# Four small moves in a two-block transformer kernel: modulation tiles over more slabs, context steps that take turns with banks, low parts one step later, head sums inside a gate's product

## The chip, the cores and the metric

The kernel runs on one core of a Trainium2 chip. The metric is the device time of one execution in microseconds (us), as a median over runs.

## The reference

The reference runs two blocks one after the other, in float32, for 512 tokens of width 1024. What matters here, cut to its core:

```python
# first block, layer l of 2: 256 context tokens beside 512 latent ones
mod_lat = silu(c) @ w_ada[l] + b_ada[l]             # six shift/scale/gate vectors; the same for ctx
h = modulate(rms_norm(x, g_mix[l]), sh1, sc1)
p = softmax(qn @ kn + qr @ kr); o_a = p @ va                      # 8 heads
p = softmax(q1 @ k1) - lam * softmax(q2 @ k2); o_b = p @ vb       # 4 heads
y_b = (rms_norm(o_b, g_sub) * (1 - lam_init)) @ w_br_b
merged = sigmoid(ga) * (o_a @ w_br_a) + sigmoid(gb) * y_b         # two gates
x = x + gate * (merged @ w_out);  x = x + gate2 * conv_ffn(h2, p)
# second block, layer l of 2: projections, scores of an index, then
o_a = attention over the 256 best keys                            # 8 heads, causal
o_b = gated linear attention;  o_c = pools
x = x + concat(o_a, o_b, o_c) @ w_out;  x = x + conv_glu_ffn(...)
```

In layer 0 of the first block context queries attend to the 256 context keys, and latent queries to all 768. In layer 1 there are latent queries only.

## The kernel before

**Weights.** All weights stream from HBM as slabs of 128 x 1024, in the order of use. A slab is split into a high and a low part, and a product is three matmuls (`product`, L677 to L679). The high part is ScalarE's (`split_high`, L1461), the low part VectorE's (`split_low`, L2054). There are two places for raw slabs and two for split ones: slab n is split when slab n-2 has been used. SyncE's queue issues the loads.

**Order.** The five engines have programs written out by hand, and meet on semaphores. TensorE is in order, and so are VectorE and ScalarE: a wait holds up all that stands behind it.

**Modulation.** The vectors `mod` for later stages are sums over rows of `ada_w`, made on VectorE tile by tile (`ada_tiles`, L2240: one instruction for each tile and vector). `ADA_AFTER` says how many tiles stand behind the low split of which slab of layer 0; slabs 15 to 18 are used in the first attention, 19 to 22 in the token-major product that makes `vB` behind it. ScalarE copies `vB` out only when the whole group is done (`mod_ready`). Two more groups lie in the down products of layer 0's feed-forward, one in each half: 32 tiles of one vector, then 16 of two. There `BOTH_DOWN` = 11 slabs are used, and a group is dealt out over the closings of slabs by `len * closed // (BOTH_DOWN - 4)`.

**First block's attention** (`attend2`; `attn_a` with two maps for a step, `attn_b` with one difference). Layer 0 has 24 steps each: for each of four heads or pairs, two context steps of 256 keys, and four steps of 768. Scores lie in PSUM banks 0 and 1 for the first map, 2 and 3 for the second. A step: scores on TensorE (L1036 to L1041, L1064), minima on VectorE (L2381), exponentials on ScalarE (L1641), scaling on VectorE (L2413, L2432 to L2435), turning on TensorE (L994), values. Between them TensorE computes pieces of other products (`fills`). `next_scores` lets the next scores start only when both exponentials of this step are done.

**Head sums** (`mixed`, behind the second attention). ScalarE squares the four heads of `o_b`; TensorE sums them (`norm_sums`, L721, matmuls with one column) between the first and the second gate product; VectorE and ScalarE make the reciprocal roots while the second gate product runs; TensorE spreads them (`norm_spread`, L732), two heads at a time. ScalarE's order is gate 0, root, gate 1, high parts of two heads.

**Second block's attention** (`dsa`). 16 steps: four pairs of heads, four row tiles each with 1 to 4 key tiles. Behind each four steps the finished pair is split: ScalarE `high` (L1949), VectorE `mix_low` (L2131). Turning is L1362, values L1373, minima L2835, scaling L2842 and L2845, the copy out L2851.

Of the kernel before, what the change touches and what calls it, by code (L numbers as in the profile page):

```python
# [17 lines left out]
P = 128  # L18
# [41 lines left out]
BANK = 512  # L60
# [57 lines left out]
ADA_AFTER = {**{n: 2 for n in range(2, 8)}, 8: 1, 9: 1, **{n: 2 for n in range(10, 15)}, 21: 5, 22: 3}  # L118
# [109 lines left out]
def steps_of(l):  # L228

    ctx = [(P * t, CTX) for t in range(CTX // P)] if l == 0 else []  # L230
    return [(j, c, nk) for j in range(4) for c, nk in ctx + [(CTX + P * t, TOK) for t in range(QT)]]

# [89 lines left out]
def build(nc, wstream, ada_w, c_in, params, x_in, rope_tab, pos_in, cnt_in, ada_first, c_cols, out):  # L322
# [3 lines left out]
    with ctx:  # L326
# [255 lines left out]
        def _(sp):  # L582
# [47 lines left out]
            for group, first in ((2, DOWN_AT[0]), (3, DOWN_AT[1])):  # L630
                load_turns(end // RAW_SLOTS, first // RAW_SLOTS)
                ahead, tiles, n = first + RAW_SLOTS, len(ADA_GROUPS[group]), 0
                end = -(-(ahead + BOTH_DOWN) // RAW_SLOTS) * RAW_SLOTS
                for g in range(first // RAW_SLOTS * RAW_SLOTS, end):
                    reload(g // RAW_SLOTS, g % RAW_SLOTS)
                    if g == ahead:
                        load_c(group)
                    if g >= ahead:
                        upto = ADA_SLOTS[group] + tiles * max(g - ahead - RAW_SLOTS, 0) // (BOTH_DOWN - 4)
                        for _ in range(min(upto, tiles) - n):  # L640
                            load_tile(group, n)
                            n += 1
                assert n == tiles
# [8 lines left out]
        def _(pe):  # L652
# [290 lines left out]
            def attend2(l, two, scores, values, fills):  # L943
# [22 lines left out]
                def next_scores(i):  # L966
                    if i + 1 < n:
                        pe.wait_ge(p_ready, exped.now() + 2 * (i + 1))
                        scores(steps[i + 1])
# [58 lines left out]
            def attn_a(l):  # L1028
                wait_rot()

                def scores(step):
                    j, c, nk = step
                    c -= TOK - SEQS[l]
                    for a, k0, n in pieces(nk):
                        r = slice(NOPE * a, NOPE * a + NOPE)
                        nc.tensor.matmul(ps[:, 2 * a + k0 // BANK, 0:n], qn[l][r, j, c:c + P], kn[l][r, j, k0:k0 + n],  # L1036
                                         start=True, stop=False)
                    for a, k0, n in pieces(nk):
                        h = 2 * j + a
                        r = slice(ROPE_A * (h % 4), ROPE_A * (h % 4) + ROPE_A)  # L1040
                        mm = nc.tensor.matmul(ps[:, 2 * a + k0 // BANK, 0:n], qr[l][r, h // 4, c:c + P],  # L1041
# [58 lines left out]
            def mixed(l):  # L1100
# [19 lines left out]
                gate()  # L1120
                tiles = norm_sums([(1, own_tokens(l, G))] * H_B, sumB[l])
# [34 lines left out]
            def keep_busy(times):  # L1156

                for _ in range(times):
                    nc.tensor.matmul(ps[:, IDLE_BANK, :], col("ident", 0, P), par[:, 0:BANK], start=True, stop=True)

            def chunk_norm(groups, sums, first=0, busy=True):
                tiles = [(c0 - first) // P + t for c0, n in groups for t in range(n // P)]
                sq.add(DC * len(groups))
                keep_busy(2 if busy else 0)
                chunk_sums(sums, tiles, (DC - 1) * len(groups))
                keep_busy(1 if busy else 0)
# [262 lines left out]
        def _(act):  # L1429
# [201 lines left out]
            def attend2(l, two, fills):  # L1631
# [3 lines left out]
                def exps(i):  # L1635
# [3 lines left out]
                    for a in range(2):  # L1639
                        act.wait_ge(s_max, maxed.now() + 2 * i + a + 1)  # L1640
                        nc.scalar.activation(prob[l][i % 2][:, a, 0:nk], banks(2 * a, nk), ACT.Exp, bias=st[:, a:a + 1],  # L1641
# [391 lines left out]
        def _(dve):  # L2033
# [339 lines left out]
            def attend2(l, normalise, output, fills):  # L2373
# [230 lines left out]
            def ffn_both(l):  # L2604
# [18 lines left out]
                for half in range(2):  # L2623
# [9 lines left out]
                    for m in range(DC):  # L2633
                        for t in range(m * HALF, (m + 1) * HALF):
                            if t % SLAB_TILES == SLAB_TILES - 1 and t < DC * HALF - 1:
# [6 lines left out]
                                if closed == BOTH_DOWN - 3:  # L2642
# [183 lines left out]
            def dsa(l):  # L2826
# [32 lines left out]
                for i in range(n):  # L2859
# [3 lines left out]
                    if i:  # L2863
                        out_tile(i - 1)
                        if i % QT == 0:
# [352 lines left out]
```

## Time and profile before

| | |
|---|---|
| median of 3 runs | 3587.82 us (3587.49 to 3588.64) |
| profiled execution, its own time | 3586.76 us |
| its span | 3584.9 us |
| granted TensorE clock, mean share of full speed | 0.984 |
| TensorE busy | 3448.0 us (96%) |
| VectorE busy | 2091.4 us (58%) |
| ScalarE busy | 1317.6 us (37%) |
| bytes read from HBM | 296.16 MB, 83 GB/s |

The profile shows one execution. "Busy" counts the time in which an engine had an instruction at work; a wait is the idle time ahead of an instruction, with what ended it.

### The profile page before, as it was taken

Reading aid. Unit: us, or ns where it says so; the run is one execution under the profiler, and the core shown is the slowest. Engines: PE = TensorE matmul, PEld = TensorE weight load, DVE = VectorE, ACT = ScalarE, POOL = GpSimd, SP = SyncE. Lnnn points to the kernel's source line nnn. Section 1 sums busy time; section 2 is a strip of 40 time slices with the busy share of each in tenths; the row PEclk is TensorE's granted clock in tenths of the full one; section 3 lists DMA queues with packets and bytes.
Section 4 is the critical chain, followed back from the end, with each engine's and each line's share of the span. In section 5 each row is a group of like instructions: output and inputs, shape, how many; then the busy total and the mean of one; then the engine's idle time right before and its main releaser. Section 6 shows DMA issues by size and latency. Waiting matters only on the chain.

```text
span 3584.9 us, 46029 instructions
## 1 busy us (share of the span) xinstructions
PE 3448.0 (96%) x18212; PEld 2751.1 (77%) x18212; DVE 2091.4 (58%) x3287; ACT 1317.6 (37%) x2084; POOL 124.1 (3%) x70
## 2 busy tenths in 40 slices
PE   6999999999999989999999999998999999899998
PEld 5866778878888877667777888775888887678887
DVE  5945663455575575455546665595566549656643
ACT  3444343333213313444433333435322234532222
POOL 0000000000000000000000000150000006000000
PEclk9999999999999999999999999998999999999999
DMA  6400212111351232101132233320223332123332
GB/s 257 154 18 30 71 31 88 59 55 63 116 201 65 97 120 71 42 19 42 54 94 80 95 95 103 94 83 19 83 94 94 103 102 80 36 65 94 94 100 94
DMA packets 79221, 300.56 MB, mean 84 GB/s; under 512 B 8784, under 2 KB 8912, under 8 KB 77904
## 3 DMA queue, kind: packets, MB, share of 16 engines
q1 hardware_dynamic: 77760, 291.47, 25.1%
q10 hardware_dynamic: 1296, 6.82, 0.5%
q8 instruction: 112, 1.84, 0.2%
q14 instruction: 53, 0.43, 0.0%
HBM read 296.16 MB, written 2.10 MB: 83 GB/s over the span
## 4 chain that ended last, share of the span: by engine, by line
PE 87%; DVE 6%; ACT 3%; DMA 2%; issue 1%; SPq 0%; DVEq 0%; ACTq 0%
PE ps L677 23%; PE ps L679 23%; PE ps L678 23%; PE ps L994 2%; PE ps L1036 2%; PE ps L1041 1%; PE ps L1064 1%; PE ps L1050 1%; PE ps L1071 1%; PE ps L939 1%; DVE ps L2240 1%; PE ps L940 1%; PE ps L941 1%; DVE ada_o L2240 1%; PE ps L695 1%
## 5 line engine op out<-in xcount | busy, mean ns | idle before, releaser
L2054 DVE TENSOR_TENSOR split<-raw,split 128x1024 fp32r<-128x1024 f32 x412 | 504.3, 1224 | 817.4 <-ACT split L1461 816.5
L1461 ACT ACTIVATE split<-raw 128x1024 fp32r<-128x1024 f32 x442 | 466.2, 1055 | 759.8 <-PE ps L679 672.0
L677 PE MATMUL ps<-h,split 128*128 128x512 f32 x1328 | 532.6, 401 | 3.5 <-DVE split L2054 2.3
L679 PE MATMUL ps<-h,split 128*128 128x512 f32 x1328 | 524.7, 395 | 0.0
L678 PE MATMUL ps<-h,split 128*128 128x512 f32 x1328 | 524.5, 395 | 0.0
L677 PE MATMUL ps<-h_hl,split 128*128 128x512 f32 (+1 forms) x776 | 295.2, 380 | 14.2 <-DVE h_hl L2134 8.7
L677 PEld LDWEIGHTS ps<-h,split 128*128 128x128 f32 x1328 | 250.6, 189 | 69.8 <-issue 7.4
L678 PEld LDWEIGHTS ps<-h,split 128*128 128x128 f32 x1328 | 250.7, 189 | 60.1 <-issue 3.4
L679 PEld LDWEIGHTS ps<-h,split 128*128 128x128 f32 x1328 | 250.6, 189 | 58.4
L679 PE MATMUL ps<-h_hl,split 128*128 128x512 f32 (+1 forms) x776 | 277.5, 358 | 0.0
L678 PE MATMUL ps<-h_hl,split 128*128 128x512 f32 (+1 forms) x776 | 277.0, 357 | 0.0
L677 PE MATMUL ps<-h2w,split 128*128 128x256 f32 (+1 forms) x704 | 239.0, 339 | 3.1 <-DVE split L2054 2.0
L678 PE MATMUL ps<-h2w,split 128*128 128x256 f32 (+1 forms) x704 | 238.3, 339 | 0.0
L679 PE MATMUL ps<-h2w,split 128*128 128x256 f32 (+1 forms) x704 | 238.0, 338 | 0.0
L677 PE MATMUL ps<-g_hl,split 128*128 128x512 f32 x528 | 208.4, 395 | 0.0
L679 PE MATMUL ps<-g_hl,split 128*128 128x512 f32 x528 | 208.4, 395 | 0.0
L678 PE MATMUL ps<-g_hl,split 128*128 128x512 f32 x528 | 208.4, 395 | 0.0
L677 PEld LDWEIGHTS ps<-h_hl,split 128*128 128x128 f32 x776 | 150.5, 194 | 53.8 <-issue 20.9
L2381 DVE TENSOR_REDUCE stat<-ps 128x1 f32<-128x768 f32 (+1 forms) x160 | 128.5, 844 | 86.2 <-PE ps L1041 81.0
L2920 POOL TENSOR_TENSOR split<-raw,split 128x1024 fp32r<-128x1024 f32 x30 | 75.0, 2499 | 2911.0 <-ACT split L1461 2910.3
L679 PEld LDWEIGHTS ps<-h_hl,split 128*128 128x128 f32 x776 | 150.1, 193 | 21.8
L1641 ACT ACTIVATE prob<-ps,stat 128x768 f32<-128x768 f32 (+1 forms) x160 | 128.7, 812 | 102.9 <-DVE stat L2381 102.9
(412 smaller groups left out, 6294.3 us busy)
## 6 DMA issues: line engine op xcount, KB each, us to landing
raw<-wstream SPq DMA_DIRECT2D x442, 512.0 KB, 3.5
ada_t<-ada_w SPq DMA_DIRECT2D x80, 512.0 KB, 4.9
first_w<-ada_first SPq DMA_DIRECT2D x4, 2048.0 KB, 24.7
x<-x_in SPq DMA_DIRECT2D x1, 3072.0 KB, 12.4
x<-x_in ACTq DMA_DIRECT2D x1, 3072.0 KB, 10.9
ada_c<-c_in SPq DMA_DIRECT2D x2, 1024.0 KB, 4.8
out<-x SPq DMA_DIRECT2D x8, 256.0 KB, 2.2
par<-params SPq DMA_DIRECT2D x1, 1345.0 KB, 5.6
```

Of the source, the lines that this page charges most:

```text
L677: nc.tensor.matmul(o, wh, a[0], start=first, stop=False)
L678: nc.tensor.matmul(o, wh, a[1], start=False, stop=False)
L679: return nc.tensor.matmul(o, wl, a[0], start=False, stop=last)
L695: nc.tensor.matmul(o, col(perm, 0, P), src, start=True, stop=True).then_inc(acc_ready, 1)
L994: mm = nc.tensor.transpose(ps[:, 4 + t // 4, (t % 4) * P:(t % 4 + 1) * P], p[:, t * P:(t + 1) * P], col("ident", 0, P))
L1036: nc.tensor.matmul(ps[:, 2 * a + k0 // BANK, 0:n], qn[l][r, j, c:c + P], kn[l][r, j, k0:k0 + n], start=True, stop=False)
L1461: nc.scalar.activation(split[:, n % SPLIT_SLOTS, 0, :], raw[:, n % RAW_SLOTS, :], copy).then_inc(hi_split, 1)
L1641: nc.scalar.activation(prob[l][i % 2][:, a, 0:nk], banks(2 * a, nk), ACT.Exp, bias=st[:, a:a + 1], scale=-1.0, accum_out=st[:, 2 + a:3 + a ...
L2054: nc.vector.tensor_tensor(split[:, n % SPLIT_SLOTS, 1, :], raw[:, n % RAW_SLOTS, :], split[:, n % SPLIT_SLOTS, 0, :].bitcast(F32), ALU.sub ...
L2240: ins = nc.vector.tensor_tensor_reduce(out=ada_out if group == 1 else banks(6, D), in0=w, in1=ada_c[group][:, j, :], scale=1.0, scalar=0.0 ...
L2381: nc.vector.tensor_reduce(st[:, a:a + 1], banks(2 * a, steps[i][2]), AX.X, ALU.min).then_inc(s_max, 1)
L2920: nc.gpsimd.tensor_tensor(split[:, n % SPLIT_SLOTS, 1, :], raw[:, n % RAW_SLOTS, :], split[:, n % SPLIT_SLOTS, 0, :].bitcast(F32), ALU.sub ...
```

## The change

Five edits, none of which adds or takes away an instruction:

- `ADA_AFTER`: slabs 17 to 20 get one tile each, slab 21 goes from 5 tiles to 2, slab 22 from 3 to 2. In the down products the divisor goes from 7 to 8, so that each group is dealt out over one more slab. The first three `keep_busy` matmuls of `chunk_norm` write bank 4 (`ACC_BANKS`) in place of bank 6.
- `odd(step)`: the second context step of each pair writes its scores one bank higher, and its scores wait for one step's exponentials fewer.
- `dsa`: `mix_low` for a finished pair stands one step later in VectorE's program.
- `mixed`: the head sums are no longer ahead of the second gate product but inside it.

```diff
-ADA_AFTER = {**{n: 2 for n in range(2, 8)}, 8: 1, 9: 1, **{n: 2 for n in range(10, 15)}, 21: 5, 22: 3}
+ADA_AFTER = {**{n: 2 for n in range(2, 8)}, 8: 1, 9: 1, **{n: 2 for n in range(10, 15)},
+             **{n: 1 for n in range(17, 21)}, 21: 2, 22: 2}
...
+def odd(step):
+
+    _, c, nk = step
+    return nk == CTX and c == P
...
-                        upto = ADA_SLOTS[group] + tiles * max(g - ahead - RAW_SLOTS, 0) // (BOTH_DOWN - 4)
+                        upto = ADA_SLOTS[group] + tiles * max(g - ahead - RAW_SLOTS, 0) // (BOTH_DOWN - 3)
...
                 def next_scores(i):
                     if i + 1 < n:
-                        pe.wait_ge(p_ready, exped.now() + 2 * (i + 1))
+                        ended = i if odd(steps[i + 1]) else i + 1
+                        if exped.n + ended:
+                            pe.wait_ge(p_ready, exped.now() + 2 * ended)
                         scores(steps[i + 1])
...
-                        mm = nc.tensor.matmul(ps[:, 2 * a + k0 // BANK, 0:n], dq[l][r, h, c:c + P], dk[l][r, h, k0:k0 + n],
+                        mm = nc.tensor.matmul(ps[:, 2 * a + k0 // BANK + odd(step), 0:n], dq[l][r, h, c:c + P], dk[l][r, h, k0:k0 + n],
...
-                gate()
-                tiles = norm_sums([(1, own_tokens(l, G))] * H_B, sumB[l])
+                def sums_of(head, first, end):
+
+                    for t in range(first, end):
+                        at = head * per + t
+                        mm = nc.tensor.matmul(ps[:, NORM_BANK, at:at + 1], sumB[l][head][:, t * P:(t + 1) * P], col("ones"),
+                                              start=at == 0, stop=at == tiles - 1)
+                    return mm
...
+                for g in G:
+                    o = open_acc(g[1])
+                    for k in range(DC):
+                        mm = product(o, w, k, cols(h_hl)(k, g), k == 0, k == DC - 1)
+                        if k == DC - 1:
+                            mm.then_inc(slab_used if g == G[-1] else acc_ready, 1)
+                        elif g == G[-1] and k >= DC - H_B:
+                            head = k - (DC - H_B)
+                            if head == 0:
+                                pe.wait_ge(var_ready, norms.now(back=1))
+                            pe.wait_ge(sq_ready, sq.now(back=H_B - 1 - head))
+                            sums_of(head, 0, per)
+                pe.wait_ge(sq_ready, sq.now())
+                sums_of(H_B - 1, 0, per).then_inc(sums_ready, 1)
                 gate()
...
-                        nc.vector.tensor_reduce(st[:, a:a + 1], banks(2 * a, steps[i][2]), AX.X, ALU.min).then_inc(s_max, 1)
+                        nc.vector.tensor_reduce(st[:, a:a + 1], banks(2 * a + odd(steps[i]), steps[i][2]), AX.X, ALU.min)\
+                            .then_inc(s_max, 1)
...
-                                end = min(len(ADA_GROUPS[group]) * closed // (BOTH_DOWN - 4), len(ADA_GROUPS[group]))
+                                end = min(len(ADA_GROUPS[group]) * closed // (BOTH_DOWN - 3), len(ADA_GROUPS[group]))
...
-                        if i % QT == 0:
+                        if i % QT == 1 and i > 1:
                             mix_low(i // QT - 1)
```

Where it moves instructions, before and after, by the order of each engine's program. Three places; line numbers after the change are higher by up to 35.

VectorE in `dsa` of layer 0, behind the first four steps, before: `p` are the maps, `mix` the heads' outputs, `mix_hl_303` the split first pair.

```order
L2851 COPY mix<-ps 128x128
L2131 TENSOR_TENSOR mix_hl_303<-mix,mix_hl_303 128x512
L2842 RECIPROCAL stat<-stat 128x2
L2845 TENSOR_SCALAR p_299<-p_299,stat 128x256 x2
L2835 ISA p_298,stat<-ps,far 128x512
```

The same place after:

```order
L2886 COPY mix<-ps 128x128
L2877 RECIPROCAL stat<-stat 128x2
L2880 TENSOR_SCALAR p_299<-p_299,stat 128x256 x2
L2870 ISA p_298,stat<-ps,far 128x512
L2870 ISA stat 128x1
L2870 ISA p_298,stat<-ps,far 128x512
L2870 ISA stat 128x1
L2886 COPY mix<-ps 128x128
L2165 TENSOR_TENSOR mix_hl_303<-mix,mix_hl_303 128x512
L2877 RECIPROCAL stat<-stat 128x2
L2880 TENSOR_SCALAR p_297<-p_297,stat 128x384 x2
```

The low part of a pair (third line from the end) now stands behind the scaling of the next step, the minima two steps on and one more copy.

TensorE in `mixed` of layer 0, between the two gate products, before: `sumB_182` to `sumB_185` are the squares of the four heads.

```order
L679 MATMUL ps<-h_hl,split 128x512
L721 MATMUL ps<-par,sumB_182 128x1 x6
L721 MATMUL ps<-par,sumB_183 128x1 x6
L721 MATMUL ps<-par,sumB_184 128x1 x6
L721 MATMUL ps<-par,sumB_185 128x1 x6
L677 MATMUL ps<-h_hl,split 128x256
```

After, at the end of the second gate product and the start of the next:

```order
L1133 MATMUL ps<-par,sumB_183 128x1 x6
L684 MATMUL ps<-h_hl,split 128x512
L685 MATMUL ps<-h_hl,split 128x512
L686 MATMUL ps<-h_hl,split 128x512
L1133 MATMUL ps<-par,sumB_184 128x1 x6
L684 MATMUL ps<-h_hl,split 128x512
L685 MATMUL ps<-h_hl,split 128x512
L686 MATMUL ps<-h_hl,split 128x512
L1133 MATMUL ps<-par,sumB_185 128x1 x6
```

The last head's sums, which release the root, now stand behind the whole second gate product in place of ahead of it.

VectorE in the first attention of layer 0, in a context step: `prob` are the maps, `ada_t` a tile of modulation weights; `ISA` with `ada_o` is L2240. Before:

```order
L2413 TENSOR_SCALAR prob_109<-prob_109,stat 128x256 x2
L2381 TENSOR_REDUCE stat<-ps 128x1 x2
L2054 TENSOR_TENSOR split<-raw,split 128x1024
L2419 COPY qn_95<-ps 128x128
L2411 RECIPROCAL stat<-stat 128x2
L2413 TENSOR_SCALAR prob_110<-prob_110,stat 128x256 x2
```

After:

```order
L2448 TENSOR_SCALAR prob_109<-prob_109,stat 128x256 x2
L2415 TENSOR_REDUCE stat<-ps 128x1 x2
L2088 TENSOR_TENSOR split<-raw,split 128x1024
L2274 ISA ada_o,mod<-ada_t_67,ada_c_64 128x1024
L2274 ISA mod 128x1
L2274 ISA ada_o,mod<-ada_t_67,ada_c_64 128x1024
L2274 ISA mod 128x1
L2454 COPY qn_95<-ps 128x128
L2446 RECIPROCAL stat<-stat 128x2
L2448 TENSOR_SCALAR prob_110<-prob_110,stat 128x256 x2
```

One tile, two vectors, now stands between a slab's low split and the copy out and scaling of the second context step, at three of the four heads, and once behind the last step.

## Rows read from the trace of the kernel before

**Rows 1.** The page's first part: busy time, share, instructions.

```profile
PE 3448.0 (96%) x18212; PEld 2751.1 (77%) x18212; DVE 2091.4 (58%) x3287; ACT 1317.6 (37%) x2084; POOL 124.1 (3%) x70
```

**Rows 2.** TensorE's waits: us in total, times, longest us.

```profile
PE ps L1362 <- DVE p L2845: 11.2, 11, 2.2
```

**Rows 3.** Stretches: length, busy of the engines, granted clock, DMA share, GB/s.

```profile
186.90:193.60 6.70, 5.96 (x26) 4.44 (x26) 2.32 (x8) 2.36 (x10) 0.00 (x0) 0.50 0.27 78
548.70:555.40 6.70, 6.70 (x32) 6.70 (x32) 1.69 (x9) 2.35 (x3) 0.00 (x0) 0.50 0.27 78
553.17:563.62 10.45, 10.45 (x59) 9.36 (x59) 0.73 (x4) 4.05 (x5) 0.00 (x0) 0.89 0.01 2
563.62:568.60 4.98, 4.98 (x34) 4.42 (x32) 4.95 (x5) 1.97 (x3) 0.00 (x0) 1.00 0.31 105
```

**Rows 4.** Timeline of `dsa`, both layers: start, us, engine, line [idle before].

```profile
2454.95 0.44 PE L1362 MATMUL ps<-par,p 128*128 128x128 f32 x2 [0.53 <-DVE p L2845]
...
2464.74 0.44 PE L1362 MATMUL ps<-par,p 128*128 128x128 f32 x2
...
2467.33 0.69 DVE L2131 TENSOR_TENSOR mix_hl<-mix,mix_hl 128x512 fp32r<-128x512 f32 x1 [2.19 <-ACT mix_hl L1949]
...
2468.81 0.66 PE L1362 MATMUL ps<-par,p 128*128 128x128 f32 x4 [2.20 <-DVE p L2845]
...
2491.08 0.44 PE L1362 MATMUL ps<-par,p 128*128 128x128 f32 x2
...
3106.91 0.44 PE L1362 MATMUL ps<-par,p 128*128 128x128 f32 x2
...
3134.39 0.44 PE L1362 MATMUL ps<-par,p 128*128 128x128 f32 x2
```

**Rows 5.** Timeline, start of layer 0's first attention.

```profile
187.64 1.22 PE L1036 MATMUL ps<-kn,qn 64*128 64x256 f32 x4 [1.62 <-ACT prob L1641]
187.82 0.62 DVE L2413 TENSOR_SCALAR prob<-prob,stat 128x256 f32<-128x256 f32 x2
...
193.55 1.59 PE L1036 MATMUL ps<-kn,qn 64*128 64x512 f32 x8
```

**Rows 6.** Timeline, the product for `vB` and the start of the second attention.

```profile
381.49 0.50 PE L939 MATMUL ps<-split,h_hl 128*128 128x512 f32 x1 [1.37 <-DVE split L2054]
...
392.39 0.70 PE L1064 MATMUL ps<-dk,dq 64*128 64x256 f32 x4 [2.24 <-ACT vB L1448]
...
396.86 1.22 PE L1064 MATMUL ps<-dk,dq 64*128 64x256 f32 x4 [2.86 <-ACT prob L1641]
...
402.28 1.56 PE L1064 MATMUL ps<-dk,dq 64*128 64x512 f32 x8
```

**Rows 7.** Modulation tiles by line: count, busy us, mean ns, idle before.

```profile
L2240 DVE CUSTOM_DVE_ANT_0 ada_o<-ada_t,ada_c 128x1024 f32<-128x1024 f32 x64 | 78.3, 1224 | 11.2 <-DMA ada_t<-ada_w 4.9 <-ACT ada_c L1552 3.6
```

**Rows 8.** Timeline, head sums and their spreads, layers 0 and 1.

```profile
544.92 6.84 PE L721 MATMUL ps<-par,sumB 128*128 128x1 f32 x48
...
553.18 1.28 ACT L1718 ACT_TABLE_LOAD   x1
...
561.86 2.84 PE L732 MATMUL ps<-par,rstd 128*128 128x128 f32 x24
...
568.77 2.84 PE L732 MATMUL ps<-par,rstd 128*128 128x128 f32 x24
...
1756.37 3.63 PE L721 MATMUL ps<-par,sumB 128*128 128x1 f32 x32
...
1772.83 1.38 PE L732 MATMUL ps<-par,rstd 128*128 128x128 f32 x10 [1.03 <-DVE oB_hl L2131]
```

**Rows 9.** Timeline, the down products of layer 0, both halves.

```profile
1001.22 0.36 PE L677 MATMUL ps<-gw_hl,split 128*128 128x256 f32 x1 [1.34 <-DVE x L2569]
...
1328.69 0.36 PE L677 MATMUL ps<-gw_hl,split 128*128 128x256 f32 x1 [3.30 <-DVE x L2569]
...
1343.68 1.47 PE L1152 MATMUL ps<-par,sumD 128*128 128x1 f32 x12 [1.47 <-DVE sumD L2173]
```

More of the change, by code:

```diff
@@ L1035, in scores @@
                         r = slice(NOPE * a, NOPE * a + NOPE)
-                        nc.tensor.matmul(ps[:, 2 * a + k0 // BANK, 0:n], qn[l][r, j, c:c + P], kn[l][r, j, k0:k0 + n],
+                        nc.tensor.matmul(ps[:, 2 * a + k0 // BANK + odd(step), 0:n], qn[l][r, j, c:c + P], kn[l][r, j, k0:k0 + n],
                                          start=True, stop=False)
@@ L1040, in scores @@
                         r = slice(ROPE_A * (h % 4), ROPE_A * (h % 4) + ROPE_A)
-                        mm = nc.tensor.matmul(ps[:, 2 * a + k0 // BANK, 0:n], qr[l][r, h // 4, c:c + P],
+                        mm = nc.tensor.matmul(ps[:, 2 * a + k0 // BANK + odd(step), 0:n], qr[l][r, h // 4, c:c + P],
                                               kr[l][r, k0:k0 + n], start=False, stop=True, tile_position=(r.start, 0))
@@ L1118, in branch_b @@
                         gemm(w, 4, 4, kept(oB_hl[l]), g, g == G[-1])
-                gate()
-                tiles = norm_sums([(1, own_tokens(l, G))] * H_B, sumB[l])
+                def sums_of(head, first, end):
[4 more added lines that the diff above has]
+                    return mm
+                per = SEQS[l] // P
+                tiles = H_B * per
+                norms.add()
+                sq.add(H_B)
+                w = open_slab()
+                for g in G:
[12 more added lines that the diff above has]
+                sums_of(H_B - 1, 0, per).then_inc(sums_ready, 1)
                 gate()
@@ L1154, in chunk_sums, with keep_busy @@
                 mm.then_inc(sums_ready, 1)
-            def keep_busy(times):
+            def keep_busy(times, bank=IDLE_BANK):
                 for _ in range(times):
-                    nc.tensor.matmul(ps[:, IDLE_BANK, :], col("ident", 0, P), par[:, 0:BANK], start=True, stop=True)
+                    nc.tensor.matmul(ps[:, bank, :], col("ident", 0, P), par[:, 0:BANK], start=True, stop=True)
             def chunk_norm(groups, sums, first=0, busy=True):
@@ L1163, in chunk_norm @@
                 sq.add(DC * len(groups))
-                keep_busy(2 if busy else 0)
+                keep_busy(2 if busy else 0, ACC_BANKS)
                 chunk_sums(sums, tiles, (DC - 1) * len(groups))
-                keep_busy(1 if busy else 0)
+                keep_busy(1 if busy else 0, ACC_BANKS)
                 norm_spread(0, len(tiles))
@@ L1640, in exps @@
                         act.wait_ge(s_max, maxed.now() + 2 * i + a + 1)
-                        nc.scalar.activation(prob[l][i % 2][:, a, 0:nk], banks(2 * a, nk), ACT.Exp, bias=st[:, a:a + 1],
+                        nc.scalar.activation(prob[l][i % 2][:, a, 0:nk], banks(2 * a + odd(steps[i]), nk), ACT.Exp, bias=st[:, a:a + 1],
                                              scale=-1.0, accum_out=st[:, 2 + a:3 + a]).then_inc(p_ready, 1)
@@ L2638, in ffn_both @@
                                     dve.wait_ge(c_ready, group + 1)
-                                end = min(len(ADA_GROUPS[group]) * closed // (BOTH_DOWN - 4), len(ADA_GROUPS[group]))
+                                end = min(len(ADA_GROUPS[group]) * closed // (BOTH_DOWN - 3), len(ADA_GROUPS[group]))
                                 ada_tiles(group, done, end - done)
                                 closed, done = closed + 1, end
-                                if closed == BOTH_DOWN - 3:
+                                if closed == BOTH_DOWN - 2:
                                     add_bias(group)
```

## The prediction

> **What bounds the kernel now.** I read the page's busy times first: TensorE is busy for 3448.0 of 3584.9 us [rows 1], so a gain can come only from its 137 us of idle time and from stretches in which it runs at half speed. Then the waits: the largest that the change touches is the turning of maps in `dsa`, which waits 11.2 us for VectorE's scaling [rows 2]. Then the granted clock of stretches: 6.7 us at 0.50 (1.2 in place of 2.4 GHz) at the start of the first attention, where TensorE was busy for 5.96 of them, and again 6.7 us behind the head sums [rows 3]. A wait that goes can thus be worth more than itself. Last the timelines around each edit [rows 4 to 9], which the sum is made from. It is made against the profiled execution (3586.76 us); the median of the runs is 1.1 us above that.
>
> **Low parts a step later: 11.5 + 1.0 us gained.** Behind four steps of `dsa` VectorE waits 2.19 us for ScalarE's high part before it makes the low one, and the next scaling is queued behind; the turning on TensorE waits 2.20 us for that [rows 4]. ScalarE makes the high part only behind its exponentials. One step later it is there. What VectorE then does in the place of the wait, scaling of step 5, needs exponentials that were done long before. The low part (0.69) stays on VectorE's path in the next step, which had 0.2 us of slack, so about 0.65 us of new delay. The first four steps, which hold no low part, give the pace: from 2454.95 to 2464.74, 9.8 us. The eight steps behind them take 26.3 us in layer 0 (2464.74 to 2491.08) and 27.5 in layer 1 (3106.91 to 3134.39) [rows 4]. Four groups at 9.8 + 0.65 are 41.8 in place of 53.8: 12.0 us, of which 6 are waits (4 x (2.2 - 0.65)) and the rest half clock behind them. If the clock falls all the same, only the 6 are left. I take 11.5, near the upper end, since the first group runs with short waits of its own at full clock. The third low part of each layer lies beside the sums of the other heads, which fill TensorE's wait already: 0.5 us each, between nothing and 2.2.
>
> **Banks in turn: 2.5 us gained in the first attention.** Only second context steps change, eight in layer 0. I went through TensorE's row in front of each: it waits only in the first pair of each attention, 1.62 us and 2.86 us [rows 5, 6]; at the other six it comes to the scores after the exponentials. So six of eight are worth nothing. In the first attention the scores then run beside the exponentials, and turning waits for the scaling that starts at 187.82 [rows 5]: it can start at about 188.2. From there the remaining pieces (12 matmuls of 256 columns, 1.4 us at full clock, and two turnings) lead to the next scores at about 190.4, where they now start at 193.55: 3.1 us. If the clock stays at half, as it does now from 186.9 [rows 3], 1.3. I take 2.5.
>
> **Modulation tiles: 5.6 us gained at the second attention, with the banks.** A tile of two vectors is 2 x 1.22 us and their steps, some 2.6 us [rows 7]. Behind slab 21's split VectorE now has five, so slab 22's low split is late and TensorE waits 1.37 us; the last tile ends late too, ScalarE copies `vB` only then, and scores wait 2.24 us; then come the 2.86 us above, partly because the low split of a slab is queued ahead of the minima [rows 6]. With two tiles each, slab 22's split ends before TensorE needs it and the group is done about 10 us (four tiles) earlier. The first scores move from 392.4 to 388.6; VectorE's queue (a copy, a high and a low split: 0.6 + 1.05 + 1.2) lets minima start at about 391.5 in place of 395.3, and the scores of the third step can start at 396.0 in place of 402.28: 6.3 us, or 4.6 if the clock falls there again. I take 5.6.
>
> **What the tiles cost where they go.** In a context step VectorE waits 1.0 us for values and has 2.7 us before its next minima; a tile of 2.6 us moves the scaling of the second context step by 1.5 us, and its turning stands behind 3 us of scores. Nothing. Queued behind the tile are the copy out and that scaling; TensorE's next value product waits for the copy 4 us later. SyncE's queue gets a tile's load between slab loads; a tile waits for the tile two before, which is used by then, and the raw slab behind it is needed 40 us later. Without that cover it would be up to 1.5 us at each of three places.
>
> **Down products: 1.3 + 2.6 us gained.** In the first half one wait of 1.34 us goes, as a slab now has 4 tiles and never 5 [rows 9]. In the second half VectorE is the pace: two or three tiles of two vectors, the split, and the residual with its sums of squares. Its work is the same, but two tiles (5.2 us) go behind the last slab that TensorE had to wait for, to where VectorE now idles 3.2 us. TensorE's wait of 3.30 goes, and the sums of squares come at 1340.1 in place of 1343.68 [rows 9]: 3.6 us. But TensorE then ends its products about 5 us ahead of those sums in place of 3, which can take the clock down for the norm behind: I take 2.6, between 0.5 and 3.6. The bank of `keep_busy` costs nothing: no one else uses bank 4 there.
>
> **Head sums: 2.2 us lost.** Now the sums end at 551.6, the table load for the next function starts at 553.18, the rest of the root is 0.7 us of VectorE, all beside the second gate product; the spread at 561.86 waits for nothing [rows 8]. In the middle lies 6.7 us at half clock [rows 3]. The sums at full clock are 0.109 us a matmul (32 in 3.49 us), so 5.2 us for layer 0. Woven in, the product (8.5 us, twice the 4.3 between the first spread's end and the second spread) and the sums end at 544.9 + 8.5 + 5.2 = 558.6. The root takes 2.4 us more: spread at 561.0, 0.8 us earlier than now. But ScalarE has gate 1 behind the root: a table load, a sigmoid, two copies and a split, 4.05 us of work [rows 3], to 564.2; then VectorE's split, scaling and low parts, 4.95 us, to 569.2, where the second spread now starts at 568.77 [rows 3, 8]. So +0.5 us; in layer 1, with a shorter product (5.6 us) and the low parts already 1.03 us late [rows 8], the same sum gives +1.6. I take 2.2, between a gain of 1 (if only the spread counted) and a loss of 4 (if the clock falls in the new gap).
> On the clock, the stretch at 0.50 behind the head sums shows TensorE busy for all of its 6.70 us, with matmuls of one column ahead of it [rows 3, 8]; so it was not idleness that took it down. The Trainium skill, "TensorE: Matmul & The Clock Gate", section "Why this matters for your kernels", names idle gaps as what to avoid. By that alone the weaving would return none of the 3.3 us that the half clock costs layer 0 now, and the loss would be 5.5 in place of 2.2; the trace speaks against it.
> On the table load, the row shows 1.28 us and the sigmoid right behind [rows 8]. The Trainium skill, "ScalarE: Activation LUTs", section "What ACT_TABLE_LOAD costs", gives about 2.66 us for a switch, with a drain. By that the loss would be 2.8 us larger over both layers; no such drain stands in this trace.
>
> **The sum.** 11.5 + 1.0 + 2.5 + 5.6 + 1.3 + 2.6 - 2.2 = 22.3 us. 3586.8 - 22.3 = 3564.5, and with the 1.1 us of the median 3565.5 us.
>
> **The rivals.** *The clock falls anyway* (0.14): `dsa` gives 6, the attentions 1.3 and 4.6, the down products 1.8, the head sums lose 4: 10 us, 3578. For it: `dsa` runs close to where the clock falls. Against: it holds through the first four steps of both layers.
> *The moves bring nothing* (0.04): the waits only move on, since `dsa`'s VectorE is the bound once the low part is on its path, and the tiles hold up attention; 3588. Against: VectorE waits several times in each group of four steps now.
> *Slower* (0.02): SyncE's queue is blocked by a tile's load in front of a slab's load in the first attention, so that TensorE runs out of slabs. It decides once it costs more than 7.4 us at each of the slabs 17 to 20 (29.5 us over four, against a gain of 22.3 and 7.2 us of margin); say 10 us each gives 3606. Against: a slab is used for some 40 us there and a load takes 3.5 to 5.
>
> **The numbers.** The forecast with its own bounds gets 0.80, 3557 to 3574. With the first rival's near side the range is 3556 to 3576 us. A measurement of this kernel can tell 0.2%, 7.2 us, from no change. Faster by more than that: 0.80 + 0.14 = 0.94; within: 0.04; slower: 0.02.
>
> **What the profile after would show.** `dsa`: no wait of 2.2 us for scaling, four steps in some 10.4 us, no half clock inside. First attention: second scores without a wait, third step's scores 3 us earlier; at the other context steps no difference. `vB`: no wait for slab 22's split, none for `vB`. Down: the last long wait for `x` gone, sums of squares 3.6 us earlier with a longer wait before them. Head sums: TensorE waits some 2.4 us for the root and 1 to 2 us for low parts. Wrong would be: half clock behind the woven sums that costs over 4 us, or VectorE late at the turnings of second context steps.

## The result and the profile after

The changed kernel takes 3553.22 us (3552.59 to 3557.43, 4 runs) against 3588.23 us (3587.49 to 3593.46) before: ratio 0.9902, 95% interval 0.9885 to 0.9919, so 29 to 41 us faster. The forecast was 3565.5 us with 3556 to 3576: the direction was right, the gain too small by 12 us, and the time lies 2.8 us below the range. The profiled executions are 33.4 us apart (3586.76 and 3553.33). Two executions on record, one of the kernel before (9248.31 us) and one of an experiment (13619.91 us), were far slower than all others and stay out of every ratio here.

The page's first part, after, answers to [rows 1]:

```profile
PE 3430.9 (97%) x18212; PEld 2738.6 (77%) x18212; DVE 2089.4 (59%) x3287; ACT 1316.8 (37%) x2084; POOL 122.6 (3%) x70
```

TensorE is busy for 17.1 us less, though its instructions are the same. It was busy for 96.2 us at half clock before and is for 58.6 after; work at half clock takes twice as long (12 matmuls of the head sums 2.55 us in place of 1.39, below), so half of the difference, 18.8 us, is what the half clock no longer takes, about the 17.1 us. The other 16 us are waits.

Timeline of TensorE after, at the starts of the two attentions, against [rows 5, 6]:

```profile
188.19 0.44 PE L1003 MATMUL ps<-par,prob 128*128 128x128 f32 x2 [0.94 <-DVE prob L2448]
...
190.22 1.56 PE L1045 MATMUL ps<-kn,qn 64*128 64x512 f32 x8
...
385.07 0.70 PE L1073 MATMUL ps<-dk,dq 64*128 64x256 f32 x4
386.61 0.70 PE L1073 MATMUL ps<-dk,dq 64*128 64x256 f32 x4
390.77 0.44 PE L1003 MATMUL ps<-par,prob 128*128 128x128 f32 x2 [1.48 <-DVE prob L2470]
392.16 1.56 PE L1073 MATMUL ps<-dk,dq 64*128 64x512 f32 x8 [0.59 <-ACT prob L1675]
```

The third step's scores stand at 190.22 in place of 193.55 (forecast: 190.4) and at 392.16 in place of 402.28. No score waits for `vB` now.

Head sums after, layer 0 and layer 1, against [rows 8]:

```profile
532.65 1.39 PE L1133 MATMUL ps<-par,sumB 128*128 128x1 f32 x12
...
539.08 2.55 PE L1133 MATMUL ps<-par,sumB 128*128 128x1 f32 x12
...
551.65 2.84 PE L739 MATMUL ps<-par,rstd 128*128 128x128 f32 x24
...
1745.36 0.95 PE L1133 MATMUL ps<-par,sumB 128*128 128x1 f32 x8
...
1751.83 1.95 PE L739 MATMUL ps<-par,rstd 128*128 128x128 f32 x16
...
1757.59 2.05 PE L739 MATMUL ps<-par,rstd 128*128 128x128 f32 x16 [1.03 <-DVE oB_hl L2165]
```

The first spread still follows a whole product behind the last sums (12.6 us after their start in layer 0, 6.5 in layer 1, with no wait). The sums are woven into the gate product that stood *ahead* of them. The text ahead of this one calls it the second gate product; that is a misreading of the diff, and the forecast rests on it.

Down products after, the waits of the second half and the norm, against [rows 9]:

```profile
1273.22 0.36 PE L684 MATMUL ps<-gw_hl,split 128*128 128x256 f32 x1 [0.97 <-DVE x L2604]
...
1296.74 0.39 PE L684 MATMUL ps<-gw_hl,split 128*128 128x256 f32 x1 [1.65 <-DVE split L2088]
...
1322.30 1.88 PE L1193 MATMUL ps<-par 128*128 128x512 f32 x4
1328.11 2.69 PE L1186 MATMUL ps<-par,sumD 128*128 128x1 f32 x12 [3.93 <-DVE sumD L2207]
1330.66 2.06 PE L1193 MATMUL ps<-par 128*128 128x512 f32 x2
```

The wait of 3.30 us for `x` is gone. Of the smaller ones, 1.57 us for a split and 0.64 for the root are gone, and one of 1.28 is down to 0.33. Behind them the wait for the sums of squares has grown from 1.47 to 3.93 us, and the sums behind it take 2.69 us in place of 1.47.

`dsa` after, layer 0, against [rows 4]:

```profile
2438.08 0.44 PE L1396 MATMUL ps<-par,p 128*128 128x128 f32 x2 [0.53 <-DVE p L2880]
...
2447.87 0.44 PE L1396 MATMUL ps<-par,p 128*128 128x128 f32 x2
...
2452.44 0.88 PE L1396 MATMUL ps<-par,p 128*128 128x128 f32 x6 [0.77 <-DVE p L2880]
...
2458.26 0.44 PE L1396 MATMUL ps<-par,p 128*128 128x128 f32 x2
...
2468.64 0.44 PE L1396 MATMUL ps<-par,p 128*128 128x128 f32 x2
```

Four steps take 10.39 us; 0.6 us late at the third step (0.77 of wait in place of 0.17) is what the low part still costs.

Stretches after (length, busy of PE, PEld, DVE, ACT, POOL, granted clock, DMA share, GB/s), against [rows 3]:

```profile
187.00:193.60 6.60, 5.66 (x39) 3.66 (x36) 2.50 (x9) 2.23 (x10) 0.00 (x0) 1.00 0.46 159
388.60:402.00 13.40, 11.32 (x64) 8.00 (x64) 8.90 (x20) 6.50 (x20) 0.00 (x0) 1.00 0.12 39
538.29:545.10 6.81, 6.81 (x32) 6.61 (x31) 2.82 (x10) 4.67 (x6) 0.00 (x0) 0.51 0.22 70
1741.40:1751.83 10.43, 10.43 (x60) 8.98 (x60) 2.73 (x10) 5.32 (x7) 0.00 (x0) 1.00 0.16 52
...
1322.30:1338.26 15.96, 10.95 (x38) 6.65 (x36) 9.76 (x20) 6.37 (x10) 0.00 (x0) 0.79 0.37 131
2438.08:2468.64 30.56, 26.43 (x228) 16.28 (x228) 24.40 (x101) 22.37 (x63) 0.00 (x0) 1.00 0.00 1
2468.64:2487.41 18.77, 15.88 (x126) 12.43 (x125) 10.28 (x31) 8.58 (x17) 0.00 (x0) 0.82 0.01 2
3101.50:3124.40 22.90, 20.07 (x134) 16.05 (x133) 11.75 (x33) 9.21 (x18) 0.00 (x0) 0.70 0.00 1
```

The clock is now full at both attentions, behind layer 1's head sums and in the first twelve steps of both `dsa` stages. In the last group of each `dsa` stage and the rows behind it, it is not (the last two rows), as before the change (0.76 and 0.71 there). It is still half behind layer 0's head sums, and newly so at the norm.

### The profile page after: what moved, and what is told of

The parts are those of the page before. It is cut to its first block, busy times and chain, and to the rows that moved or that the text cites. A ratio compares the mean times of both kernels' runs of the same rounds, so it can differ in the third digit from the quotient of the medians.

```text
span 3551.5 us, 46029 instructions
## 1 busy us (share of the span) xinstructions
PE 3430.9 (97%) x18212; PEld 2738.6 (77%) x18212; DVE 2089.4 (59%) x3287; ACT 1316.8 (37%) x2084; POOL 122.6 (3%) x70
## 4 chain that ended last, share of the span: by engine, by line
PE 89%; DVE 6%; ACT 3%; issue 1%; DMA 1%; SPq 0%; DVEq 0%; ACTq 0%
PE ps L684 24%; PE ps L686 23%; PE ps L685 23%; PE ps L1003 2%; PE ps L1045 2%; PE ps L946 1%; PE ps L1050 1%; PE ps L1073 1%; PE ps L948 1%; PE ps L947 1%; PE ps L1059 1%; PE ps L1080 1%; DVE ps L2274 1%; PE ps L702 1%; ACT split L1495 1%
## 6 DMA issues: line engine op xcount, KB each, us to landing
x<-x_in SPq DMA_DIRECT2D x1, 3072.0 KB, 12.5
```

## Experiments

Each kernel was timed beside the kernel before, and a ratio compares these two; the kernel before had medians of 3592.80 us beside the first four experiments (low parts, head sums, banks and tiles alone), 3592.64 beside the next (down products alone, the second product, nine dummies) and 3588.12 beside the last two. So the medians below are not to be held against 3588.23.

How they are read: the kernels differ by less than one timing can tell, so each trace is cut at the starts of the same TensorE instructions (before: 184.14, 205.48; 375.07, 408.40; 540.02, 575.21; 988.18, 1040.09; 1247.04, 1364.14; 1750.01, 1778.11; 2425.56, 2454.95, 2512.02; 3097.13, 3158.20), and the pieces are compared. Each piece, in us, over the profiled executions of all kernels with and without the edit in question:

```
stretch                        without the edit       with it                  forecast gain
start of the first attention   20.20-21.35 (7)        18.00-18.04 (6)          2.5
vB and second attention        33.27-33.48 (6)        banks alone 30.88; tiles
                                                      alone 26.97; both
                                                      26.53-26.60 (5)          5.6
layer 0's head sums            35.10-36.72 (6)        33.53-36.69 (6)          \ -2.2
layer 1's head sums            28.10-28.13 (6)        26.55-26.57 (6)          /
down, first half               51.89-51.92 (7)        50.09-50.17 (6)          1.3
down, second half, and norm    117.05-120.72 (7)      115.20-116.12 (3)        2.6
dsa, a group with a low part   12.17-14.57 (7 x 4)    10.38-10.39 (5 x 4)      11.5 over four
dsa, layer 0, last group       16.47-16.73 (7)        14.48 (4), 15.73         \ 1.0
dsa, layer 1, last group       17.63-18.64 (7)        17.70-17.71 (5)          /
no edit: ahead of first dsa    26.99 or 29.39-29.42 (13)
no edit: start of the program  176.78-179.88 (13)
```

The whole profiled times are no measure of one edit: 3573.89 us for low parts alone (expected 3571.5 or 3574.3), 3585.30 for head sums alone (3585.1), but 3588.49 for banks alone (3580.9) and 3585.17 for tiles alone (3577.9 to 3583.2). With banks alone the two edited stretches gave 5.8 us, as expected, while the start of the program was 2.4 us longer than in the first trace, the second half of down 3.6 and the rows from 575 to 988 us 2.6, none of them touched by that edit. The gains by single timings (18.3, 5.0, 6.5, 6.1 and 6.1 us by the ratios) add up to 42, each with an interval of 3 to 6 us to either side, too wide to tell that from the 35 of the whole change.

**Low parts alone.**

```diff
-                        if i % QT == 0:
+                        if i % QT == 1 and i > 1:
                             mix_low(i // QT - 1)
```

> Kernel before with the low parts one step later alone. If the gain seen in both dsa stages is this edit's own (in the traces of before and after the distance to the kernel before grows from 16.9 to 24.6 us in layer 0's dsa and from 26.2 to 33.8 in layer 1's): 15.3 us, 3571.5 profiled. Rival, the forecast's term: 12.5 us, 3574.3. Position theory: the first stretch at half clock (2443.0 of the kernel before) stays, since nothing ahead of it moves, and the one at 2989 goes or stays by where the stage then falls: 1.6 us more or not.

3574.52 us, ratio 0.9949 (0.9933 to 0.9966); `dsa` takes 51.56 and 53.45 us. Against the kernel before's first trace (57.07, 61.07) that is 5.5 + 7.6 = 13.1, against the mean of the seven traces without the edit (58.43, 60.19) 6.9 + 6.7 = 13.6 us: between the two numbers expected. Groups are 10.38 us each, exactly as in the changed kernel. That layer 0's stage takes 2.2 us more here than there (49.33) lies in its last group (15.73 for 14.48) and the rows behind it, at half clock for longer. From the start of the last group to the end of the stage it is 21.00 us here, 20.94 to 21.98 in the seven traces without the edit, and 18.77 to 18.78 in the two traces of the changed kernel and the two with dummies alone. So the edit alone does not show the gain that the changed kernel has there; where it comes from no run isolates.

**Head sums alone.**

```diff
-                gate()
-                tiles = norm_sums([(1, own_tokens(l, G))] * H_B, sumB[l])
+                w = open_slab()
+                for g in G:
+                    o = open_acc(g[1])
+                    for k in range(DC):
+                        mm = product(o, w, k, cols(h_hl)(k, g), k == 0, k == DC - 1)
...
+                            sums_of(head, 0, per)
...
+                sums_of(H_B - 1, 0, per).then_inc(sums_ready, 1)
                 gate()
                 norm_spread(0, tiles // 2)
```

> Kernel before with the head sums woven into the first gate product alone. If the gain belongs to this edit: 0.15 us in layer 0 and 1.55 us in layer 1 (no half clock behind the sums), 3585.1 profiled. Rival, the forecast's term: 2.2 us slower, 3589.0. Position theory: layer 1's gain depends on where the stage falls and can be 0; then 3586.6.

3587.86 us, ratio 0.9986 (0.9976 to 0.9996). Layer 0: 35.14, no gain; layer 1: 26.56, 1.55 us gained, as in all six traces with the edit. That is neither the forecast's loss nor chance: 28.10 to 28.13 without, 26.55 to 26.57 with. In the kernel before, the stretch behind those sums ran at 0.76:

```profile
1759.86:1767.07 7.21, 7.21 (x26) 5.75 (x26) 1.60 (x9) 2.13 (x3) 0.00 (x0) 0.76 0.19 73
```

The matmuls of one column stood in a row of 32 for 3.63 us [rows 8]; in pieces of 8 with products between, the clock holds (1.00 above). In layer 0, with pieces of 12, it falls as before. Why it holds in the one and falls in the other no run isolates.

**Head sums in the second gate product**, which is what the forecast had costed:

```diff
                 gate()
-                tiles = norm_sums([(1, own_tokens(l, G))] * H_B, sumB[l])
-                gate()
+                w = open_slab()
+                for g in G:
...
+                sums_of(H_B - 1, 0, per).then_inc(sums_ready, 1)
                 norm_spread(0, tiles // 2)
```

> Kernel before with the head sums woven into the second gate product, which is what the forecast had costed. By its working: 0.5 us lost in layer 0 (stretch of 35.2 us to 35.7), 1.7 lost in layer 1 (28.1 to 29.8), between a gain of 1 and a loss of 4. Rival: the root then stands in front of the spread with no cover, and the clock falls in the wait: 4 us or more lost.

3596.84 us, ratio 1.001 (1.000 to 1.002). Layer 0 39.79 us, 4.6 lost; layer 1 29.56, 1.45 lost: 6.1 us in both, against 2.2 forecast and 4 as its worst. TensorE's timeline, both layers, ScalarE's in layer 1, and a stretch of layer 0:

```profile
553.20 1.39 PE L1124 MATMUL ps<-par,sumB 128*128 128x1 f32 x12
555.25 2.55 PE L1124 MATMUL ps<-par,sumB 128*128 128x1 f32 x12
559.09 2.55 PE L1124 MATMUL ps<-par,sumB 128*128 128x1 f32 x12
563.96 5.26 PE L732 MATMUL ps<-par,rstd 128*128 128x128 f32 x24 [2.31 <-DVE rstd L2141]
...
1774.54 0.95 PE L1124 MATMUL ps<-par,sumB 128*128 128x1 f32 x8
1777.70 3.41 PE L732 MATMUL ps<-par,rstd 128*128 128x128 f32 x16 [2.21 <-DVE rstd L2141]
```
```profile
1776.83 1.28 ACT L1743 ACT_TABLE_LOAD   x1
1778.12 0.63 ACT L1743 ACTIVATE ga<-ga 128x512 f32<-128x512 f32 x1
```
```profile
555.20:568.90 13.70, 11.39 (x51) 10.96 (x50) 2.92 (x10) 4.05 (x6) 0.00 (x0) 0.50 0.01 2
```

The wait for the root is 2.31 and 2.21 us (forecast: 2.4), and layer 1's loss is the forecast's within 0.2 us. In layer 0 the costing fell short by 4.1. The clock did not fall in the new gap, as the forecast had feared, but 6.4 us ahead of it: at 555.2 us, with TensorE busy for all of 555.2 to 561.6 us, and it stayed at half for 13.7 us in place of 6.8 [rows 3]. The third and the fourth head's sums took 2.55 us each in place of 1.39, the product between them was slow too, and they ended at 561.6 and not at 558.6, and the spread behind the gap took 5.26 us in place of 2.84. In layer 1 the clock did fall in the gap (at 1777.2 us, for 3.4 us), but the fall that the kernel before has ahead of it did not come, so that the number agrees there partly by luck. The costing of the wait was sound, then, and that of the clock was not, on the place that it was meant for too.

**Banks alone** (`odd` and all its uses):

```diff
-                        pe.wait_ge(p_ready, exped.now() + 2 * (i + 1))
+                        ended = i if odd(steps[i + 1]) else i + 1
+                        if exped.n + ended:
+                            pe.wait_ge(p_ready, exped.now() + 2 * ended)
```

> Kernel before with banks in turn alone. First attention: 3.4 us earlier, as in the trace of the changed kernel. Second attention: the wait of 2.86 us goes, but minima still stand behind the copy of vB, so 2.5 us: together 5.9, 3580.9. Rival: without the tiles moved the banks bring nothing at the second attention, since minima are late: 3.4, 3583.4.

3585.93 us, ratio 0.9982 (0.9972 to 0.9992). First attention 18.02, second 30.88 (2.45 gained, as expected). The first attention without banks has two lengths, 21.35 and 20.20, by how long the clock stays at half; with them it has one. The edit is worth 2.2 to 3.3 us there.

**Tiles alone** (`ADA_AFTER`):

```diff
-ADA_AFTER = {**{n: 2 for n in range(2, 8)}, 8: 1, 9: 1, **{n: 2 for n in range(10, 15)}, 21: 5, 22: 3}
+ADA_AFTER = {**{n: 2 for n in range(2, 8)}, 8: 1, 9: 1, **{n: 2 for n in range(10, 15)},
+             **{n: 1 for n in range(17, 21)}, 21: 2, 22: 2}
```

> Kernel before with the modulation tiles over slabs 17 to 22 alone. The waits of 1.37 and 2.24 us at the vB product go; the wait of 2.86 and the half clock behind it stay: 3.6 us, 3583.2. If the clock does not fall there: 5.3 us more at most, 3577.9. Rival: tiles in attention cost something at the second context steps, up to 1.5 us at each of three: 3586 to 3588.

3586.56 us, ratio 0.9983 (0.9973 to 0.9992). The stretch takes 26.97 us: 6.4 us gained without banks. The wait for the exponentials stays, but the half clock behind it does not come:

```profile
393.31 0.70 PE L1065 MATMUL ps<-dk,dq 64*128 64x256 f32 x4 [2.74 <-ACT prob L1642]
```
```profile
385.00:400.00 15.00, 12.26 (x69) 9.07 (x68) 6.81 (x15) 6.92 (x18) 0.00 (x0) 1.00 0.18 63
```

The kernel with banks alone has it the other way round: its first two waits stay (1.53 and 2.34 us), the last is 0.59, and the clock over 385 to 400 us is 0.89. So here it fell behind the first waits, not behind the last. That rests on one trace of each kernel; that both edits together keep the clock full, on five. Banks add 0.4 us to the tiles. The rest of the first attention, in which tiles now stand, takes 169.6 to 169.8 us in all thirteen traces, with and without them: the zero that was forecast for them holds.

**Down products alone** (divisor 8, and bank 4 for the dummies):

```diff
-                                end = min(len(ADA_GROUPS[group]) * closed // (BOTH_DOWN - 4), len(ADA_GROUPS[group]))
+                                end = min(len(ADA_GROUPS[group]) * closed // (BOTH_DOWN - 3), len(ADA_GROUPS[group]))
```

> Kernel before with the divisor 8 in the down products and bank 4 for the first dummy matmuls alone. By the trace of the changed kernel: first half 1.8 us shorter (stretch of 51.9 us to 50.1), second half with its norm 1.8 shorter (117.1 to 115.3), as the 6.1 us gained ahead of the norm are partly given back at half clock behind a wait of 3.9 us. Rival: the giving back is chance of position, and here the whole second half comes out 3 us or more shorter. Time ratio 0.999 against the kernel before.

3585.82 us, ratio 0.9983 (0.9974 to 0.9993). First half 50.17, second 116.12. The wait of 4.01 us and the slow sums behind it are there too:

```profile
1339.63 2.69 PE L1152 MATMUL ps<-par,sumD 128*128 128x1 f32 x12 [4.01 <-DVE sumD L2173]
```

How much the norm gives back depends on what it is held against. From the start of these sums to the end of the stretch it is 20.46 us in the first trace of the kernel before, where the clock fell nowhere in the stretch, but 20.44 to 22.43 (mean 21.28) in the seven traces without the edit, five of which have a fall of their own; with the edit it is 22.22 to 23.01 (mean 22.50, three traces). On the means the norm gives back 1.2 us of the 4.5 gained ahead of it. The bank of the dummies stands in the same kernel and was not tried by itself.

**The same programs again.** The kernel before and the changed kernel, each unchanged:

> The kernel before, unchanged, once more with a profile. Position theory: stretches that no edit touches differ between executions of one program by 1 to 3 us each where the clock falls or not (the stretch ahead of the first dsa stage 27.0 or 29.4; dsa of layer 0 57 to 60; dsa of layer 1 59 to 61). Rival: each program has its own fixed lengths; then every stretch comes within 0.3 us of the first profile.

> The changed kernel, unchanged, once more with a profile. If its 33 us hold two or three us of chance: stretches without an edit move by 1 to 3 us (start of the program 176.9 to 179.9; ahead of the first dsa stage 27.0 or 29.4), while the edited ones stay: first attention 18.0, product for vB and second attention 26.5, layer 1's head sums 26.6, groups of four steps in dsa 10.4. Rival: everything within 0.3 us of the first profile.

3589.24 and 3553.53 us. The kernel before, again: start of the program 179.88 (176.95 at first), first attention 20.21 (21.34), second half of down 119.82 (117.10), ahead of `dsa` 26.99 (29.39), `dsa` 59.25 and 59.99 (57.07 and 61.07). So identical instructions differ by 1 to 3 us where the clock falls or not. The runs were made on several chips, but that does not explain it: on one of them the start of the program, the same in all kernels, took 176.83 us with low parts alone and 179.53 with head sums alone. The stretch ahead of `dsa`, first and second trace of the kernel before:

```profile
2435.37:2454.95 19.58, 18.39 (x233) 12.71 (x233) 9.54 (x24) 10.88 (x19) 0.00 (x0) 0.83 0.07 27
```
```profile
2438.00:2457.76 19.76, 17.15 (x237) 11.70 (x236) 11.98 (x27) 13.00 (x23) 0.00 (x0) 1.00 0.10 29
```

The changed kernel's second trace is much like its first: all edited stretches within 0.1 us, an unedited one (behind the head sums) by 1.0, another by 1.4.

**Dummies in the new wait.** Nine and, in a second kernel, four, on top of the changed kernel:

```diff
+                    keep_busy(9, ACC_BANKS)
                     chunk_norm(BOTH, sumD)
```

> Changed kernel with nine more dummy matmuls in the wait of 3.93 us for the sums of squares behind the second down half. If the half clock behind that wait comes from the idle time: the clock stays at 1.00 and the norm is 1.8 us shorter (stretch of 33.3 us to 31.5 or less), as long as the dummies (9 x 0.43 = 3.8 us) end before the sums are there. Rival: the dummies run past the sums or the clock falls anyway: 0 to 1 us longer.

> Changed kernel with four more dummy matmuls (0.86 us each, as the run with nine showed, 3.4 us in all) in the wait of 3.93 us. If idle time takes the clock down there: stretch of the second down half with its norm 115.3 us to 113.4. Rival: the dummies load the clock too little, or the clock falls all the same: 115.3, no change. Over the whole kernel 1.9 us at most, at the edge of what the timing can tell.

Nine: the second half with its norm 117.14 us (115.27 without), since a dummy takes 0.86 us and not 0.43, and they ran 3.7 us past the sums; even so only 1.9 were lost, as the clock stayed full. Four: 113.40 us, 1.9 gained, to the number expected:

```profile
1326.17 5.31 PE L1194 MATMUL ps<-par 128*128 128x512 f32 x12
1332.04 1.47 PE L1187 MATMUL ps<-par,sumD 128*128 128x1 f32 x12 [0.56 <-DVE sumD L2208]
```
```profile
1326.17:1341.00 14.83, 12.56 (x48) 6.69 (x47) 10.44 (x21) 6.44 (x10) 0.00 (x0) 1.00 0.41 141
```

The run below has the same four dummies and was traced too, and there the gain is mostly gone: 114.75 us, 0.5 less than without. The clock fell all the same, at 1335.7 us, 2.4 us after the start of the sums and with no wait over 0.63 us since the last product:

```profile
1336.40 2.93 PE L739 MATMUL ps<-par,rstd 128*128 128x128 f32 x12 [0.63 <-DVE rstd L2151]
1339.12 4.42 PE L1194 MATMUL ps<-par 128*128 128x512 f32 x6
```

So with the wait unfilled the clock fell in three traces of three, with it filled in one of three. That speaks for the idle time as a cause, which agrees with what the Trainium skill, "TensorE: Matmul & The Clock Gate", section "Why this matters for your kernels", says of gaps; it does not show it, and filling the wait is no sure cure. The whole kernels take 3556.82 and 3555.51 us, no difference that the timing can tell.

**Low parts in the long step**, with the four dummies:

```diff
-                        if i % QT == 1 and i > 1:
+                        if i in (7, 11, 13):
```

> Changed kernel with the four dummies and with the low parts of dsa behind steps 7, 11 and 13 in place of 5, 9 and 13. If the low part finds slack in the long fourth step of a group: the wait of 0.77 us behind the third step goes and the four groups take 9.8 us in place of 10.4, 2.4 us in all. Rival: the low part is in VectorE's way in any step: 10.4 again.

All four groups take 9.79 us (the third low part of a layer stays behind step 13); the third step waits 0.17 again:

```profile
2453.85 0.88 PE L1397 MATMUL ps<-par,p 128*128 128x128 f32 x6 [0.17 <-DVE p L2881]
```

The last group of layer 0 took 15.38 in place of 14.48, so 1.7 us show in the two stages (49.60 and 51.48 for 49.33 and 53.45). 3552.70 us, ratio 0.9894 (0.9877 to 0.9910): the lowest median here, and against the changed kernel's own ratio not to be told from it.

## Why the prediction missed

The profiled gain of 33.4 us by stretch, and what was forecast:

- **Head sums, +1.6 for -2.2.** The step that failed: "Woven in, the product ... and the sums end at 544.9 + 8.5 + 5.2 = 558.6". The product that now holds the sums is the one that ended at 544.9 already. The root keeps its cover and nothing is lost: that is 2.2 us of the miss. The other 1.6 are layer 1's half clock, which the forecast had not looked at. A second premise failed with it: the weaving was to give back the half clock of layer 0 (sums at 5.2 us, "3.3 us that the half clock costs layer 0 now"). It gave back nothing there (35.13 us for 35.18, the clock at 0.51 over 6.81 us); it did in layer 1. So the reading that the prediction set against its own, that weaving returns nothing, came true in layer 0 and failed in layer 1. Read rightly, with no loss, the same range would have begun at 3553.8, still 0.6 us above the measured time; only with layer 1's 1.6 us as well, at 3552.2, would it have held it. So this step is the largest part of the miss and not all of it.
- **Low parts, +12.3 for +11.5, and +3.1 for +1.0.** The mechanism and its price were right: 9.8 + 0.6 for a group, no half clock inside. Mis-sized was the third low part, taken as 0.5 a layer: its group is 2.0 and 0.9 shorter. How much of that is the edit's own stays open, since the edit alone does not show layer 0's part. Over many traces the groups' gain is 12.5 us (mean 13.5 without the edit).
- **Tiles and the second attention, +6.8 for +5.6.** The place was right (392.16 against the forecast 396.0 less the 3.3 us of the first attention), the reason partly not: "with the banks" was wrong, tiles alone give 6.4. Its upper end was 6.3.
- **Banks, first attention, +3.3 for +2.5.** The clock did not fall at all; the working's own full-clock end was 3.1. On the means it is 2.7, since the first trace of the kernel before had the longer of two lengths.
- **Down, +1.8 for +1.3, and +1.8 for +2.6.** The sums of squares came 3.6 us earlier, to the number forecast, and the clock loss that was named as a risk came and took 1.8 back. On the means of all traces 1.2 of 4.5 us are given back and the second half gains 3.3.
- **No edit, +2.7 for 0.** 2.4 us ahead of the first `dsa` and 1.6 between the two stages, less 1.3 elsewhere. One execution of the kernel before had them and another did not: its second trace has 26.99 and 583.60 us there, the changed kernel's values (26.99 and 583.54), where the first had 29.39 and 585.11. So they are no sure effect of the change. The forecast's sum was made against a trace with such chances in it and did not allow for any.

Taking for each edited stretch the mean of all traces without and with the edit, the five edits give 2.7 + 6.8 + 1.6 + 1.8 + 3.3 + 8.6 + 6.7 = 31.5 us, inside the timed 29 to 41. Against 22.3 the miss is 9.2 us: 3.8 in the head sums, 2.8 in `dsa`, 1.2 each at the second attention and in the down products, 0.2 at the first attention. The timed gain is 35.0 us; the 3.5 us between the two are within its interval and are put down to no edit.

The rival "the clock falls anyway" was wrong in the first twelve steps of `dsa`, the attentions and layer 1's sums, right at the norm. "The moves bring nothing" lies outside the timed 29 to 41 us. That of slab loads held up by tiles was wrong: 169.6 to 169.8 us throughout. In the changed kernel the table load stands under a product and costs nothing. In the kernel with the sums in the second product it is not covered, and there it takes the 1.28 us of its row, 0.02 us behind the root and with the sigmoid 0.01 us behind it: no drain stands in this trace either, and the longer switch that the prediction named beside its sum is not seen.

## What to carry to other kernels

Before costing a moved instruction, name what stands between it and the next one that waits, before and after: one look at the product ahead of the spread would have shown that it keeps its cover. Where several waits stand close together, the half clock behind them can go with the first of them, as it did in one kernel here; and small work is worth trying in the longest slack step rather than one step on. Take several traces of an unchanged kernel before summing microseconds from one, and of a fix that rests on the clock too: the four dummies gave 1.9 us in one trace and 0.5 in the other.

## What the runs showed of the hardware

- The clock's falls are not a property of the program alone: with the same instructions, the stretch ahead of the first `dsa` took 26.99 us in ten traces (26.98 to 27.00) and 29.4 in three, nothing between; two traces of the kernel before have one of each.
- A long product has two paces. The same 1200 matmuls from 1969 us on took 278.86 us (nine traces, 278.85 to 278.87) or 280.00 us (four: the kernel before again, the changed kernel, the one with four dummies and the one with the second product), 0.4% apart; the changed kernel has 280.00 in its first trace and 278.86 in its second. 800 of them in the second block took 185.90 us in all thirteen.
- A dummy matmul of float32 with 512 columns is two records of 0.43 us each, 0.86 us in all.
- The clock was at half behind layer 0's head sums for 6.7 us with TensorE busy throughout, before [rows 3] and after (0.51 over 6.81 us). The last wait ahead of it was 0.47 us, 13 us before the clock fell in both traces, so idle time is not the only thing that takes it down.
